# FFN columns of a mixture-of-experts layer in three parts of 3, 4 and 4 blocks in place of four parts of 2, 3, 3 and 3

## The reference, cut to what matters

```python
def moe_swiglu(h, router, wg, wu, wd):
    logits = (h @ router).astype(jnp.float32)
    top_v, top_i = lax.top_k(logits, TOP_K)          # 2 of 8 experts for each token
    gates = jax.nn.softmax(top_v, axis=-1)
    out = jnp.zeros_like(h)
    for e in range(N_EXPERTS):
        gate_e = jnp.sum(jnp.where(top_i == e, gates, 0.0), axis=-1)[..., None].astype(h.dtype)
        out = out + gate_e * swiglu(h, wg[e], wu[e], wd[e])   # (silu(h@wg) * (h@wu)) @ wd
    return out
```

## Time and profile before

| | us |
|---|---|
| median of 3 runs | 1392.17 (1391.61 to 1392.94) |
| the profiled execution | 1397.93 |
| its span | 1396.2 |
| PE busy | 1335.8, 96% of the span |
| DVE, ACT, POOL busy | 371.4, 177.9, 61.4 |
| the stage of the experts, first weight transfer issued | 664.1 |

### The profile page before, as it was taken

How to read it: one execution, slowest core, us unless ns; L and a number is a source line. 1 busy time by engine, 2 the same in 40 slices (tenths; PEclk the granted TensorE clock), 3 DMA queues, 4 the chain that set the end, 5 groups by cost and what they waited for, 6 DMA issues and landing times.

```text
span 1396.2 us, 18086 instructions
## 1 busy us (share of the span) xinstructions
PE 1335.8 (96%) x7651; PEld 850.7 (61%) x7651; DVE 371.4 (27%) x825; ACT 177.9 (13%) x376; POOL 61.4 (4%) x87
## 2 busy tenths in 40 slices
PE   6999998999999999989999999999999999999976
PEld 5888887888888888758755434334343343344432
DVE  3535885421111017933200011101111011010102
ACT  1231424010001001042100000010000100000002
POOL 2003210000000102000000000000000000000000
PEclk9999999999999999999999999999999999999998
DMA  8536722564546333410999999999999999999993
GB/s 263 205 123 234 265 91 91 181 202 127 177 148 212 98 121 121 128 43 16 358 402 402 402 398 399 393 402 394 405 391 402 403 392 404 387 393 403 391 404 157
DMA packets 169666, 381.48 MB, mean 273 GB/s; under 512 B 7660, under 2 KB 63516, under 8 KB 169530
## 3 DMA queue, kind: packets, MB, share of 16 engines
q1 hardware_dynamic: 161571, 358.96, 69.3%
q0 software_dynamic: 3184, 11.40, 2.7%
q10 hardware_dynamic: 4834, 9.99, 2.2%
HBM read 372.41 MB, written 9.01 MB: 273 GB/s over the span
## 4 chain that ended last, share of the span: by engine, by line
PE 88%; DMA 6%; SPq 2%; DVE 2%; ACT 1%; issue 1%; ACTq 0%; DVEq 0%
PE ps L1711 34%; PE ps L2179 15%; PE ps L2244 11%; PE ps L2194 8%; PE ps L2204 4%; DMA big<-in_moe_w_up_dram 3%; PE ps L1937 3%; PE ps L2255 2%; DMA region<-in_moe_w_down_dram 1%; PE ps L2000 1%; SPq L593 1%; PE ps L2136 1%; PE ps L2147 1%; PE ps L2221 1%; DMA big<-in_w_in_even_dram 1%
## 5 line engine op out<-in xcount | busy, mean ns | idle before, releaser
L1711 PE MATMUL ps<-big 128*128 128x264 f32 x1376 | 314.6, 391 | 4.1 <-DMA big<-in_w_in_even_dram 4.1
L1711 PEld LDWEIGHTS ps<-big 128*128 128x128 f32 x1376 | 264.3, 193 | 50.6 <-DMA big<-in_w_in_even_dram 4.2
L2179 PE MATMUL ps<-big,region 128*64 128x384 f32 (+3 forms) x1200 | 219.6, 462 | 10.8 <-DMA big<-in_moe_w_up_dram 7.0
L2179 PEld LDWEIGHTS ps<-big,region 128*64 128x64 f32 (+1 forms) x1200 | 114.3, 148 | 111.6 <-issue 65.3
L1711 PE MATMUL ps<-region,big 128*128 128x264 f32 x704 | 160.0, 390 | 3.7 <-ACT region L965 3.7
L2244 PE MATMUL ps<-big,region 128*64 128x512 f32 (+1 forms) x608 | 154.6, 598 | 2.6 <-DMA big<-in_moe_w_down_dram 2.1
L1711 PEld LDWEIGHTS ps<-region,big 128*128 128x128 f32 x704 | 134.5, 192 | 27.2 <-issue 4.1
L2194 PE MATMUL ps<-big,region 128*64 128x384 f32 (+1 forms) x720 | 111.7, 461 | 2.8 <-DMA big<-in_moe_w_gate_dram 1.5
L2244 PEld LDWEIGHTS ps<-big,region 128*64 128x64 f32 (+1 forms) x608 | 49.8, 143 | 93.1 <-issue 89.0
L2194 PEld LDWEIGHTS ps<-big,region 128*64 128x64 f32 x720 | 51.4, 137 | 60.0 <-issue 47.9
L1626 DVE TENSOR_TENSOR region<-region,ps 128x384 f32<-128x384 f32 (+1 forms) x24 | 12.2, 520 | 231.7 <-PE ps L2179 231.7
(11 more groups left out here) (373 smaller groups left out, 1017.3 us busy)
## 6 DMA issues: line engine op xcount, KB each, us to landing
big<-in_moe_w_up_dram SPq DMA_DIRECT2D x48, 1536.0 KB
big<-in_moe_w_gate_dram SPq DMA_DIRECT2D x40, 1536.0 KB
big<-in_moe_w_down_dram SPq DMA_DIRECT2D x40, 1536.0 KB
big<-in_w_in_even_dram SPq DMA_DIRECT2D x10, 2048.0 KB
big<-in_moe_w_gate_dram SPq DMA_DIRECT2D x16, 1024.0 KB
big<-in_moe_w_up_dram SPq DMA_DIRECT2D x16, 1024.0 KB
big<-in_moe_w_down_dram SPq DMA_DIRECT2D x16, 1024.0 KB
region<-in_moe_w_gate_dram SPq DMA_DIRECT2D x8, 1536.0 KB
```

Source lines behind the costliest of these rows:

```text
L1711: ins = mm(ps[:, 0:T], w[:, c, cols:cols + P], src[:, c, :], start=c == 0, stop=c == nk - 1)
L2179: ins = mm(out, xg[:, 4 * j + c, 0:cap], w[:, c, r, :], start=j + c == 0, stop=j + c == 4)
```

## The change

`DBLK` has three parts of 3, 4 and 4 blocks. Up matmuls of the last two parts are 512 columns wide. An expert is 18 pieces of 3 or 4 units. The ring has 34 units: pieces 0 to 9 take the places 0 to 33, pieces 10 to 17 begin at place 0 again and take 32 of them. `big` and `region` become views of one tensor `both`, so that a piece may lie across the border; SP's first wait for the old contents moves from piece 11 to piece 7. The order on PE becomes:

up 0, turn the gates, up 1, turn 0, down 0 with the scatter, up 2, turn 1, down 1, turn the next item's rows, turn 2, down 2.

```diff
-PIECES = 24
-RING_PIECES = 13
-RING_UNITS = 33
-BIG_UNITS = 30
+PIECES = 18
+RING_PIECES = 10
+RING_UNITS = 34
...
-DBLK = ((0, 2), (2, 5), (5, 8), (8, 11))
+DBLK = ((0, 3), (3, 7), (7, 11))
+THIRDS = len(DBLK)
...
-UP_ORDER = (0, 4, 10, 14)
-DOWN_ORDER = (8, 18, 20, 22)
+UP_ORDER = (0, 4, 10)
+DOWN_ORDER = (8, 14, 16)
...
-        starts.append(at % RING_UNITS)
+        at = 0 if n == RING_PIECES else at
+        starts.append(at)
...
-GATE_DONE = (3, 7, 13, 17)
-UP_DONE = (4, 8, 14, 18)
+GATE_DONE = (3, 7, 13)
+UP_DONE = (4, 8, 14)
...
+        item["gather"] = use(4, 5)
         item["T2"] = use(4) if cap == 64 else use(4, 5)
-        item["gather"] = use(4, 5)
-        item["T3"] = use(5) if cap == 64 else use(4, 5)
...
-        sgm = (reg(14976, 384), reg(19904, 384))
+        sgm = (reg(14976, 512), reg(19904, 512))
...
-            n = 1024 * UNITS[at]
-            if STARTS[at] >= BIG_UNITS:
-                return region[:, 0:n]
-            return big[:, 1024 * STARTS[at]:1024 * STARTS[at] + n]
+            return both[:, 1024 * STARTS[at]:1024 * (STARTS[at] + UNITS[at])]
...
-                    elif at == 11:
+                    elif at == 7:
                         filled(sp, ("xt2", 5))
...
                 load_up(10, 2)
-                load_up(14, 3)
-                load_down(18, 1)
-                load_down(20, 2)
-                load_down(22, 3)
+                load_down(14, 1)
+                load_down(16, 2)
...
                         n = MULS[s] + reps * k + r
-                        if n >= 2:
+                        if s == STATIC and not k:
+                            act.wait_ge(sem("moe_mul"), t * XMULS + n)
+                        elif n >= 2:
                             act.wait_ge(sem("moe_mul"), t * XMULS + (n - 1))
...
                 columns(1)
-                silu(3)
+                moe_xg(SEQ_CAP[min(s + 1, EXP - 1)], t * STEP4 + USES[s]["gather"][0])
                 columns(2)
-                moe_xg(SEQ_CAP[min(s + 1, EXP - 1)], t * STEP4 + USES[s]["gather"][0])
-                columns(3)
...
                 turn_act(1)
-                up(3, 14)
-                turn_act(2)
-                down(1, 18)
+                down(1, 14)
                 turn_rows_in(SEQ_CAP[min(s + 1, EXP - 1)], t * 16 + 16 * (s + 1), t * STEP4 + USES[s]["gather"][0],
                              t * STEP5 + USES[s]["gather"][1], s >= STATIC)
-                turn_act(3)
-                down(2, 20)
-                down(3, 22)
+                turn_act(2)
+                down(2, 16)
```

More of the change, by code:

```diff
@@ L52, in piece_table @@
     for n in range(PIECES):
-        starts.append(at % RING_UNITS)
+        at = 0 if n == RING_PIECES else at
+        starts.append(at)
         at += units[n]
-    assert starts[RING_PIECES] == 0 and at == 2 * RING_UNITS
+        assert at <= RING_UNITS
     before = [range(RING_PIECES, PIECES) if n < RING_PIECES else range(RING_PIECES) for n in range(PIECES)]
@@ L210 @@
 STEP5 = USES[EXP]["start"][1] - USES[EXP - 1]["start"][1]
-XMULS = 4 * REPS[SEQ_CAP[EXP - 1]]
-MULS = [sum(4 * REPS[SEQ_CAP[k]] for k in range(s)) for s in range(EXP + 1)]
-MIDS = [sum(4 * (SEQ_CAP[k] == 96) for k in range(s)) for s in range(EXP + 1)]
+XMULS = THIRDS * REPS[SEQ_CAP[EXP - 1]]
+MULS = [sum(THIRDS * REPS[SEQ_CAP[k]] for k in range(s)) for s in range(EXP + 1)]
+MIDS = [sum(THIRDS * (SEQ_CAP[k] == 96) for k in range(s)) for s in range(EXP + 1)]
 def build(nc, i, o):
@@ L236, in build @@
                 sem(s)
-        big = sb("big", 32256)
+        both = sb("both", 32256 + 20800)
+        big = both[:, 0:32256]
         ring = big[:, 0:24576]
@@ L258, in build @@
         row16 = sb("row16", 16, parts=1)
-        region = sb("region", 20800)
+        region = both[:, 32256:32256 + 20800]
         def reg(at, n):
@@ L1650, in moe_item @@
                 multiply(2)
-                multiply(3)
                 moe_xg(SEQ_CAP[min(s + 1, EXP - 1)], t * STEP5 + USES[s]["gather"][1])
```

## The result

Over 20 runs of each kernel the changed one takes 1397.93 us (median), the one before 1393.86; the ratio is 1.0032, 95% interval 1.0023 to 1.0041, or 3.2 to 5.7 us. The forecast was +4.1 us.

A forecast was written before the change was run, and what follows sets the result against it. PE and DMA were both full, the stage ending when the last unit lands. PE's +7.3 us at item 6 became +3.2 at landing, plus 0.9 for the last piece: +4.1, 1392.2 to 1396.3 us, range 1394 to 1399.

The forecast's parts named there:

- Transfers: Expert weights, up pieces: longer runs save between 0 and 1.1 us an expert, 9 us for all.
- Turns: PE's transposes in items 0 to 5, copies exposed: +2.05 us for room 128, +3.3 for rooms 64, +4.5 for rooms 96.
- upper bound of +12: PE's change up to item 6 if every turn is as slow again as priced: +12 us.
- Start: Ahead of item 0: the first piece is a unit longer, so PE begins 1.3 us later.
- PE up to item 6: Start, turns and matmuls +10.0 us, waits for weights in item 4 gone: +7.3, item 6 begins at 1235.0 for 1227.7.
- sign of being wrong: Forecast wrong if item 6 begins before 1231, or if the DMA share stays at 1.03 there.
- Ring: At most 420 units issued until item 5 ends; transfers stand still, then 108 units remain: last landing +3.2 us.
- End: After the last landing: a last piece of 4 blocks leaves PE 16 matmuls for 12, +0.9 us.
- (b): Rival: no turn costs more than its hidden form; PE -2.6, end -5.8, 1386.4 us; chance 0.10.
- (c): Rival: bound by transfers alone, the ring never stops them; -8.2, 1384.0 us; chance 0.03.
- (a): Rival: only turn 2 is paid, turns 0 and 1 hide their copies; PE +3.3, end +0.1, 1392.3 us; chance 0.25.
- (d): Rival: standstill from the start of item 1 starves PE in item 2 by about 4 us; 1400 us; chance 0.07.

The follow-up runs named there:

- all turns inside: Changed three-part kernel with turns 0, 1 and 2 moved between the halves of up 1, up 2 and down 1: 0.9945 and, measured again, 0.9950 of before.
- warm start: Changed kernel plus 20 small matmuls on PE while it waits for the first piece: 1.0016 of before; with turns moved between halves too, 0.9952.
- turn 2 inside: Changed kernel with turn 2 moved between the halves of down 1 and the next item's row turn behind down 1: 0.9980 of before.
- four-part kernel with exposed turns: Kernel before with PE's order alone changed, turns 1, 2 and 3 each directly ahead of their down part: 1.0060 of before.
- four-part one with all turns inside: Kernel before, its pieces, ring and runs kept, with all four turns moved between the halves of an up or down part: 1.0000 of before.

## Why the prediction was right

**Transfers: right.** 409 GB/s in 4-block up pieces; the forecast of 9 us less in all is not seen in after, but with all turns inside the last piece of the three-part kernel lands 8.7 us before that of the four-part one (703.6 for 712.3), and both are bound mostly by transfers there. The estimate by the Trainium skill's rule (DMA: Bandwidth & Descriptors, Why small descriptors are slow), about 3 cycles for each descriptor, was 4 us in all; the traces have about twice that, also where the runs are parts of longer lines.

**Turns: the mechanism right, the sum too high.** The exposed turns are 1.34 and 1.32 us in rooms of 64 (forecast 1.42), 1.78 and 1.63 in rooms of 96 (1.9 and 1.7), and 1.82 and 1.85 in the room of 128 (1.85). PE's time for items 0 to 5 was to grow by 8.75 us with turns and matmuls, and grew by 3.8 (differences of the items' lengths, the clock's 1.8 in item 0 and the 2.8 of waits for weights in item 4 left out). The room of 128 has +1.9 for 1.9, rooms of 64 +0.8 for 1.5, rooms of 96 +0.3 in items 2 and 5 and -0.4 in item 4 for 1.3 each; why item 4 differs is open. Two terms were mis-sized. Up parts of 4 blocks save more in rooms of 96, where a block costs 5.30 us of them (half a part takes 10.59) and 5.35 in a part of 3 (half a part 8.03): with the narrow part that goes, 0.7 an item where I had 0.2, as I had read the cost of a block in a room of 64 only. And I overlooked a line of the change: turn 2 in a room of 64 now uses bank 4, which ACT frees, where turn 3 used bank 5, which DVE frees later; the wait ahead of it is 0.34 us and was 0.74:

```profile
848.59 0.52 PE L2221 MATMUL ps<-ident,region 128*128 128x128 f32 x3 [0.74 <-DVE region L1572]
```

The upper bound of +12 does not follow from the terms either: all turns twice as dear give +17. What was measured is far below both.

**Start: right in size, with a cost I had not seen.** Item 0 begins 9.5 us after the first issue for 8.2 (+1.3). PE's wait of 3.14 us, 1.8 before, was followed by a fall of its clock, and the first part took 22.57 us for 20.81, the time of such a part at full clock with the warm start and in the earlier trace rows (20.64 leaves out the end of the last matmul), so 1.8 more:

```profile
670.00:676.00 6.00, 5.70 (x13) 3.24 (x14) 0.00 (x0) 0.00 (x0) 0.00 (x0) 0.72 1.03 412
```

**PE up to item 6: +4.1 for +7.3.** The prediction's own sign of being wrong was an item 6 before 1231. As written it came true (1228.5); counted from the first issue, which was 3.3 us earlier in this execution, item 6 begins at 1231.8 on before's scale, just past the edge. And the +4.1 holds 1.8 us of a fallen clock, for which the sum had no term.

**Ring: right.** The standstill, the three pieces at item 5's end, and the last landing 145.2 us after item 6's start (712.9 - 567.7) where the sum had 144.3. Where PE is the late one this holds in the other three-part kernels too: 145.4 with the warm start and with turn 2 inside. In the four-part kernel with exposed turns it is 143.2; the same sum with 27 units out, so 105 left, gives 105 x 0.5243 / 0.398 + 2.5 + 1.0 = 141.8. In before the distance is 148.4, so of the +4.1 at item 6 only +0.9 reaches the last landing, as the sum had +3.2 for +7.3.

**End: too low, which made up for it.** After the last landing I gave PE 0.9 us more than before; it took 2.6 more (718.3 - 714.8 less the 0.9 of the landing). "Items 6 and 7 on PE have slack, so their longer turns cost nothing" failed for the last turn: turn 2 and its copy stand ahead of the last down part, the weights for whose first half are there already, and PE's clock fell again (8.60 us for 7.09). So the stage no longer ends when the last piece has landed, as the prediction had it. In sum -3.2 on PE, +0.9 in what follows item 6, +1.7 at the end: the profile's stage is 3.5 us longer on PE for a forecast of 4.1, and the agreement with the runs' 4.07 is in part errors that cancel.

The two falls of the clock, 1.8 us at the start and 1.5 at the end, are in this execution of after and not in that of before. Without them the 3.5 us would be about 0.2 (an estimate: it takes the 1.8 as handed on whole). How often the clock falls there in the other executions, and so how much of the 4.07 is the clock's, no run here shows; the warm start leaves the first fall out and lies between before and after.

Of the rivals, (b) and (c) are out by the waits seen; (a), that only turn 2 is paid, comes close in PE's total (+3.3 for +4.1) but for the wrong reason, since turn 1 is exposed as well, and gives an end of +0.1. The standstill ahead of item 1 that (d) begins with did occur (a share of 0.77 from 780 to 800), the starved PE did not: its waits for weights between 672 and 1228 are gone.

## What to carry to other kernels

Where weights stream through a ring and both TensorE and the transfers are full, ask for each part size three things at once: what a longer run saves for each byte, which copy stood hidden behind the part that goes, and how many units can be out when TensorE is latest. A gain of 0.5% from longer runs was turned into a loss of 0.3% in a kernel with waits of 0.7 us for copies that had no matmuls beside them and a ring that passed PE's lateness on; setting each transpose between the halves of a neighbouring part brought it back. And a trial kernel in which one engine has less to do tells in one run which of two full engines binds.

## What the runs showed that I had not expected

A wait of PE of 3.1 us ahead of item 0 (after) was followed by a clock of 0.72 over 6 us and 1.8 us of longer matmuls; with matmuls in that wait the clock stayed at 1.00. In before the wait at this place was 1.8 and the clock stayed at 2.4 GHz. The length of this wait does not settle it: in the four-part kernel with exposed turns it was 1.90 us and the clock fell (0.72 from 670 to 676), in the four-part one with all turns inside 1.94 us and it did not. What decides is not shown.

The changed kernel's transfers stand still as much ahead of item 1, behind the room of 128, as at item 5's end.
